# A gated delta layer of sixteen heads, worked in groups of four beside the next group's projections, with VectorE making the low parts of its weights

## The reference, cut to what matters

```python
def gated_delta_net(h, w_in, conv_w, a_log, dt_bias, norm_w, w_out):
    proj = h @ w_in
    qkv, z, b, a = jnp.split(proj, GDN_SPLITS, axis=-1)
    qkv = jax.nn.silu(causal_depthwise_conv(qkv, conv_w))
    ...
    q = l2_norm(q.reshape(B, T, GDN_K_HEADS, GDN_HEAD_DIM)) * GDN_HEAD_DIM ** -0.5
    k = l2_norm(k.reshape(B, T, GDN_K_HEADS, GDN_HEAD_DIM))
    ...
    o = chunk_gated_delta_rule(q, k, v, g, beta)
    o = rms_norm_2(o, norm_w) * jax.nn.silu(z.reshape(B, T, GDN_V_HEADS, GDN_HEAD_DIM))
    return o.reshape(B, T, GDN_V_W) @ w_out
```

## Time and profile before

| what | us |
|---|---|
| median of 3 runs | 3005.7 (3003.59 to 3010.06) |
| the profiled execution | 3002.97 |
| its span | 3001.2 |
| granted TensorE clock, mean | 0.909 |
| TensorE busy | 2625.9 (87%) |
| VectorE busy | 1721.6 (57%) |
| ScalarE busy | 1188.9 (40%) |
| GpSimd busy | 505.7 (17%) |
| HBM read | 340.86 MB, 114 GB/s over the span |

### The profile page before, as it was taken

The page is one execution under the profiler, slowest core; times in us unless marked ns, Lnnn a source line. Parts: engine busy times, 40 slices in busy tenths (PEclk is TensorE's granted clock), DMA queues, the critical chain, the costliest instruction groups (busy, mean ns, idle before and its releaser), DMA issues. The chain is left out here.

```text
span 3001.2 us, 49678 instructions
## 1 busy us (share of the span) xinstructions
PE 2625.9 (87%) x19342; PEld 2485.9 (83%) x19342; DVE 1721.6 (57%) x2747; ACT 1188.9 (40%) x1956; POOL 505.7 (17%) x400
## 2 busy tenths in 40 slices
PE   6998998996989788998999946989988788888998
PEld 6998888995987678997999844889888677778898
DVE  3677784665655444665566763466585733324665
ACT  2533554443444324442444442344444422223443
POOL 1110690000652000000000030000054221221000
PEclk9999799997999888999999966799998888878999
DMA  4465003553435421552455411235533200003453
GB/s 160 146 209 189 1 1 113 168 190 109 140 129 168 106 36 57 192 186 86 147 190 180 159 52 37 94 121 189 173 120 128 90 1 1 1 1 106 130 185 98
DMA packets 107153, 344.26 MB, mean 115 GB/s; under 512 B 20433, under 2 KB 26161, under 8 KB 106481
## 3 DMA queue, kind: packets, MB, share of 16 engines
q1 hardware_dynamic: 106992, 342.07, 35.2%
HBM read 340.86 MB, written 1.16 MB: 114 GB/s over the span
## 5 line engine op out<-in xcount | busy, mean ns | idle before, releaser
L134 PE MATMUL ps<-h_high,hi 128*128 128x256 f32 x2936 | 848.2, 289 | 59.9 <-DVE h_low L272 38.1
L111 DVE TENSOR_TENSOR lo<-raw,hi 128x1024 fp32r<-128x1024 f32 x537 | 655.6, 1237 | 321.1 <-ACT hi L101 320.6
L135 PE MATMUL ps<-h_low,hi 128*128 128x256 f32 x2936 | 838.9, 286 | 0.0
L136 PE MATMUL ps<-h_high,lo 128*128 128x256 f32 x2936 | 838.7, 286 | 0.0
L101 ACT ACTIVATE hi<-raw 128x1024 fp32r<-128x1024 f32 x623 | 646.4, 1054 | 463.8 <-PE ps L136 451.0
L134 PEld LDWEIGHTS ps<-h_high,hi 128*128 128x128 f32 x2936 | 571.7, 195 | 68.1 <-DVE h_low L272 41.6
L135 PEld LDWEIGHTS ps<-h_low,hi 128*128 128x128 f32 x2936 | 571.8, 195 | 2.0 <-issue 1.7
L136 PEld LDWEIGHTS ps<-h_high,lo 128*128 128x128 f32 x2936 | 571.4, 195 | 0.0
L134 PE MATMUL ps<-hidden_h,hi 128*128 128x256 f32 x1056 | 299.4, 284 | 9.8 <-DVE lo L111 9.4
L135 PE MATMUL ps<-hidden_l,hi 128*128 128x256 f32 x1056 | 298.0, 282 | 0.0
L136 PE MATMUL ps<-hidden_h,lo 128*128 128x256 f32 x1056 | 297.8, 282 | 0.0
(11 more groups left out here) (426 smaller groups left out, 4496.1 us busy)
## 6 DMA issues: line engine op xcount, KB each, us to landing
raw<-in_weights SPq DMA_DIRECT2D x623, 512.0 KB, 3.5
at_bias<-bias_group SPq DMA_DIRECT2D x64, 64.0 KB, 2.6
s_bn<-in_s_bn SPq DMA_DIRECT2D x4, 512.0 KB, 4.3
consts<-in_consts SPq DMA_DIRECT2D x1, 1794.5 KB, 8.8
x<-in_x SPq DMA_DIRECT2D x1, 1024.0 KB, 4.9
s_cT<-in_s_b SPq DMA_DIRECT2D x1, 1024.0 KB, 7.2
s_cw<-in_s_c SPq DMA_DIRECT2D x1, 1024.0 KB, 9.2
s_cT<-s_rows SPq DMA_DIRECT2D x16, 64.0 KB, 2.8
```

Of the source, the lines that this page charges most:

```text
L111: engine.tensor_tensor(k.lo[:, item % CUT, :], k.raw[:, item % RAW, :], k.hi[:, item % CUT, :].bitcast(F32), ALU.subtract)\
L134: pe.matmul(out, wh, xh, start=start, stop=False, **more)
L135: pe.matmul(out, wh, xl, start=False, stop=False, **more)
L136: return pe.matmul(out, wl, xh, start=False, stop=stop, **more)
```

## The change

`conv_silu`, `gdn_gates`, `L2Norms`, `head_norms` and the block of `delta_rule` become one block, `gdn_heads`. The weights are laid out in the order of `gdn_order()`: the 8 items of queries, keys and values of group 0 first, then 12 items for each of groups 0 to 2 (the next group's 8, and 4 for this group's z), then 4 for group 3. Only the first 8 are worked ahead of the delta rule. The other 40 are given out in the code by `some(fill, n)`, which issues the next n tiles of the projections (`KT` is 8, so an item, or half of one) between the delta rule's steps. VectorE takes every output tile (`taken`: `mixed` with the convolution, 5 instructions, or `gate`, 1) and makes every low part (`cut`). The query and key norms are folded into the columns of the decays (`columns`) as logarithms. The output norms are taken a group at a time inside the next group. Sizes, the arithmetic of a product, and the delta rule's matmuls stay.

```diff
+def gdn_order():
+    def mixed(g):
+        return [2 * g, 2 * g + 1, KT + 2 * g, KT + 2 * g + 1] + [GH + 4 * g + i for i in range(4)]
+    order = mixed(0)
+    for g in range(4):
+        order += (mixed(g + 1) if g < 3 else []) + [2 * GH + 4 * g + i for i in range(4)]
+    return order
...
-        @block.gpsimd
-        def _(pool):
-            for n in range(nt):
-                cut_item(k, pool, first + n)
...
+        def projected(a, b):
+            for m in range(a, b):
+                if m >= 8:
+                    pe.wait_ge(g.read, m - 1)
+                elif m >= 4:
+                    pe.wait_ge(g.read, m - 3)
+                for j in range(KT):
+                    mm = product(pe, k.ps[:, out_bank(m), 0:T], w.tile(m * ITEM + j), pair_tile(k.hp, j), start=(j == 0), stop=(j == KT - 1))
+                    if j == KT - 1:
+                        mm.then_inc(k.item_used, 1)
+                    yield
...
+        for hg in range(NG):
+            fill = projected(fill_at(hg), z_end(hg))
+            pe.wait_ge(g.cg, hg + 1)
...
+            some(fill, KT)
+            pe.wait_ge(g.v, hg + 1)
+            for a in range(2):
+                pe.wait_ge(g.t, U + a + 1)
+                pe.wait_ge(g.re, U + a + 1)
...
+                if a == 0:
+                    some(fill, KT)
             for l in levels:
...
+                some(fill, KT)
+                if hg and l == 3:
...
+                    head_sums(hg - 1)
+                if hg and l == 5:
+                    head_rows(hg - 1)
...
+            some(fill, KT // 2)
             for n in range(4):
...
+                    mm.then_inc(g.ws, 1)
+                    some(fill, KT // 2)
+                    pe.wait_ge(g.vn, 3 * hg + n)
...
+                if n == 1 and hg < NG - 1:
+                    square_sums(hg + 1)
+                some(fill, KT // 2)
+        head_sums(NG - 1)
+        head_rows(NG - 1)
...
+        def mixed(m):
...
+            dve.wait_ge(k.item_used, first + m + 1)
+            tapped(dve.tensor_tensor(cin[:, m % 2, 3:], k.ps[:, out_bank(m), 0:T], k.rs[:, 0, :], ALU.mult))
+            for s in range(4):
...
+                if s == 0:
+                    tapped(dve.tensor_scalar(acc, x, wc, None, ALU.mult))
+                elif s < 3:
+                    tapped(dve.scalar_tensor_tensor(acc, x, wc, acc, ALU.mult, ALU.add))
+                else:
+                    dve.scalar_tensor_tensor(dst, x, wc, acc, ALU.mult, ALU.add).then_inc(g.read, 1)
...
             for l in levels:
...
+                if hg and l == 4:
+                    head_variance(hg - 1)
+                if hg and l == 6:
+                    gates_scaled(hg - 1)
+                if more or l < 4:
+                    taken(F + l)
+                if l > 1 and (more or l < 6):
+                    cut(F + l - 2, F + l - 1)
+                if hg and l == 5:
+                    head_inverse(hg - 1)
...
+            if more:
+                taken(F + 7)
+                cut(F + 5, F + 6)
             for n in range(4):
...
+                if more:
+                    taken(F + 8 + n)
+                    cut(F + 6 + n, F + 7 + n)
```

More of the change, by code:

```diff
@@ L2018, with some @@
 LEVELS = 6
+def gdn_order():
[5 more added lines that the diff above has]
+    return order
+def some(fill, n):
+    for _ in range(n):
+        next(fill, None)
 def gdn(k):
     nc = k.nc
[L2023 to L2048, removed]
@@ L2049, in gdn @@
+    with ExitStack() as outer:
+        v = outer.enter_context(nc.sbuf_tensor("gdn_v", [P, GH, T], F32))
+        with ExitStack() as ctx:
+            gdn_heads(k, ctx, v)
         with nc.sbuf_tensor("gdn_vh", [P, 2 * KT, T], F32R) as vh, nc.sbuf_tensor("gdn_vl", [P, 2 * KT, T], F32R) as vl:
             linear(k, (vh, vl), 2 * KT, KT, parts=(Parts(k, v, (vh, vl), 2 * KT),), leave=True)
[L2053 to L2126, removed]
@@ L2335, in delta_rule, with gdn_heads @@
-def delta_rule(k, col, qk, v):
+def gdn_heads(k, ctx, v):
     nc = k.nc
@@ new lines, in gdn_heads, with four, q_of @@
+    v0, a0, i0 = V.n, A.n, k.side_here.n
+    prep = Prep(k, VEC_AT["norm_mix_pre_2"] + KT, Prep.POST, VEC_AT["norm_ffn_post_2"])
+    block = ctx.enter_context(nc.Block())
+    ident, cum = const(k, "ident"), const(k, "cumulate")
+    lmask = const(k, "levels").rearrange("p (l n) -> p l n", l=LEVELS)
+    dmask = const(k, "decay_mask")
+    levels = range(1, LEVELS + 1)
+    def four(bank):
+        return k.ps[:, bank, :].rearrange("p (h n) -> p h n", h=HG)
+    def q_of(hg, kh):
+        return qk[:, HG * (hg % 2) + kh, :]
@@ L2412, in _ @@
                     rows = slice(a * P, (a + 1) * P)
-                    if a == 0 and hg:
-                        pe.wait_ge(g.oc, 4 * hg)
+                    pool.wait_ge(g.re, U + a + 1)
                     for kh in range(2):
-                        for half, rhs in enumerate((k_of(hg, kh), q_of(hg, kh))):
-                            pe.matmul(k.ps[:, a, (2 * kh + half) * P:(2 * kh + half + 1) * P], k_of(hg, kh)[:, rows], rhs[:, rows],
-                                      start=True, stop=True)
@@ L2659, in build @@
+            for n in (1, 2):
+                pool.wait_ge(g.s, 3 * hg + n)
+                end = (n + 1) * GC
+                pool.tensor_tensor(Sd[:, :, :], S[:, n % 2, :, :], spread(rx[:, :, end - 1:end], 2, P), ALU.mult).then_inc(g.sd, 1)
+    A.n += 5
+    k.side_here.n += 48
+    k.used += n_out
 def build(nc, ins, x_in, out, plan, n_items):
```

1019 lines of the change are left out of this document (559 added, 460 removed).

## The result

| what | before | after |
|---|---|---|
| median, 4 runs each, same chip | 3007.07 (3003.59 to 3010.06) | 2920.24 (2913.36 to 2922.55) |
| the profiled execution | 3002.97 | 2921.78 |
| its span | 3001.2 | 2919.8 |
| granted TensorE clock, mean | 0.909 | 0.917 |
| TensorE, VectorE busy | 2625.9, 1721.6 | 2597.6, 1720.6 |

The ratio is 0.9708, 95% interval 0.9687 to 0.9728: 87 us less, where the prediction said 69 (it counts from the profiled execution, which lost 81). It lies in its range and in the case held likeliest. All of it is in the layer: of the profiled spans, 86.3 us fewer there and 4.9 more in the rest together. What stands ahead of the delta rule fell from 178.3 us to 39.2 (139.1 fewer). The four groups grew by 68.8 together, since 40 items and the norms of the heads now lie in them, and the tail fell from 30.1 to 14.2.

A forecast was written before the change was run, and what follows sets the result against it. Levels were held bound by TensorE, chunk steps by a serial chain on a slow TensorE. Front 42, groups 96.3, 198.6 and 87, tail 14, clock 18, contention 6: 461.9 against 531.3, so 2934 us; range 2905 to 2985.

The forecast's parts named there:

- the case held likeliest: The prediction's own case for the whole kernel: layer 461.9 against 531.3 us, time 2934; chance 0.52.
- contention: Groups: VectorE's low parts, both operands in SBUF, slowed beside GpSimd; 0 to 7 us a group, 2 taken, 6 in all.
- wait for the inverse: Level 5 to 6: TensorE waits 2.6 us as VectorE takes the norms' inverse behind updates, tile and low part.
- The path of TensorE: Groups 1 and 2 at full clock: TensorE's work from start to chunk steps summed to 99.3 us a group.
- +6 us for the clock: Chunk steps, groups 0 to 2: 5.6 us at half clock behind outputs and column sums; 6 a group, 18 in all.
- rival of cold steps: Chunk steps stay at the low clock in all groups, 24 us a group instead of 6: time 2988; chance 0.11.
- Waits of 1.1 a group: Chunk steps: 1.1 us of waits counted within their 29.8 us at full clock.
- The slack of 1.4 us: Levels 2 to 5: VectorE free 5.2 us after a level's last product, first needed 6.6 after it.
- The table loads: ScalarE: loads go from 8 to 22, at 1.28 us; by the skill's 2.66 a switch, about 5.5 us longer.
- Clock up: Rival: the clock stays up through the groups, saving the 18 us taken for it: time 2916; chance 0.17.
- Nothing hidden: Rival: VectorE's longer queue gives back to waits what items take out; layer 499 us, time 2971; chance 0.13.
- Slower: Rival: clock down through chunk steps and next starts, adding 54 and 42 us: time 3030; chance 0.05.

The follow-up runs named there:

- inverse-first run: Changed kernel with VectorE's inverse and ScalarE's root ahead of level 5's tile, low part and rounding: median 2915.9 us, 0.9694 of the kernel before; layer 436.8 against 445.0.
- bare steps: Changed kernel with the chunk steps' items moved in a row ahead of them: median 2970.5 us, 0.9869 of the kernel before; layer 495.0 against 445.0.
- twice-in-levels run: Changed kernel with the low part made twice in levels 2 to 4 of every group only: median 2922.9 us, 0.9705 of the kernel before; layer 447.6 against 445.0.
- twice-cut run: Changed kernel with every low part in the groups made twice, 2 to 8 us longer expected: median 2957.8 us, 0.9809 of the kernel before; layer 34 us longer.
- run with the items behind: Changed kernel with all items of a group behind its chunk steps, none between steps: median 3034.0 us, 1.0075 of the kernel before; layer 556.6 against 445.0.

## Why the prediction was right, and where it was off

**The sum.** 461.9 was predicted for the layer, 445.0 measured, 16.9 too much; the rest of the program took back 5 (2469.9 before, 2474.8 after, by the profiled spans). That the profiled time came within 12 us of 2934, and not 17, is luck. By parts:

| part | predicted | measured |
|---|---|---|
| front | 42 | 39.3 |
| group 0, with clock and contention | 104.3 | 99.3 |
| groups 1 and 2, each | 107.3 | 102.9 |
| of it: start | 14.2 | 14.1 |
| a level with its item | 8.45 | 8.30 |
| wait for the inverse | 2.6 | 2.2 |
| u, w and chunk steps | 33.7 + 6 | 38.5 |
| contention | 2 | 0 |
| group 3 | 87 | 86.5 |
| tail | 14 | 14.2 |

**The path of TensorE** was right to 0.2 us a level. Levels, start and tail came as summed, and the one new wait came where it was put, 2.2 for 2.6. The inverse-first run took it away whole.

**The chunk steps**, +6 us for the clock: right in kind and nearly in size. Clock 0.85, near the 0.8 that was said, down behind outputs and column sums and back with the next half item. But the prediction had one stretch of 5.6 us at half speed, and there are two, of 6.7 and 3.4, the second behind outputs alone; by them some 5 us are lost. The bare steps show the other side: steps at 0.58. They don't price the rival of cold steps, whose items stay in the steps: of their 16.8 a group, 11.5 are items moved out of cover, so that this is near that rival's 18 is chance. The Trainium skill (TensorE: Matmul & The Clock Gate, What's actually happening) has the clock follow how busy TensorE was; by the busy time of the records the trace still disagrees, since the steps at 0.85 were busy 33.37 of 33.37 us.

**Contention**, 2 us a group: this term was wrong. It was put on VectorE's low parts from the earlier trace rows. That instruction itself still takes 1.28 once a group, as before the change. Of the layer's low parts only three were slowed, to 1.36, 1.36 and 1.77 us. In the levels it is GpSimd that gives way: its masks start behind VectorE's low part, and two of them last 3.04 us where two alone are 2.14 (GpSimd's timeline, the same level as above):

```profile
2363.34 3.04 POOL L2707 TENSOR_TENSOR dr_mt<-dr_aq,consts 128x512 f32<-128x512 f32 x2 [1.93 <-PE ps L2287]
```

They are still in time, so nothing is paid. The Trainium skill (SBUF — State Buffer, SBUF: two separate sides) has the port that the two engines share go, for a whole instruction, to the one that starts first, the other waiting. The rows agree: the low part of 1.22 began 0.19 us before the mask, and the one of 2.00 during it. The twice-in-levels run shows that even a hit VectorE stays within the slack.

**The rest.** Waits of 1.1 a group that were kept for the chunk steps did not come, and the front was 2.7 shorter than VectorE's serial count.

**The slack of 1.4 us**, on which hiding rested, was right for the place it was worked out for (1.5 to 1.9 idle in the trace, and a whole further low part hidden). It was the expectation of the twice-cut run, not the prediction, that took it for the whole group, and it failed by 26 us or more. The prediction's own argument would have stood better with a slack for each part: none in the steps.

**The table loads.** A load takes 1.28 us and the next function starts 0.01 after it; the load itself starts 0.02 after the copy ahead of it has ended. The Trainium skill (ScalarE: Activation LUTs, What ACT_TABLE_LOAD costs) counts 2.66 a switch, which by the prediction's estimate would have made the layer 5.5 longer. The trace disagrees: the tail, with two loads in it, came at 14.2 for 14.

**The rivals.** Clock up (2916): the time was nearer to it than to 2934 in the profiled execution, yet the chunk steps show 0.85, not 1.0. What brought it near was the contention, the waits and the front, each put too high. Nothing hidden (2971): the run with the items behind comes nearest to that case, and its layer is 556.6 where the rival had 499. The rival left out that a row of items starts at the lower clock and is bound by VectorE in its convolved tiles, the serial chain at each group's end, and group 3's items in the tail (14 us). Slower (3030): cold steps and cold starts did appear together, in the bare steps, and cost 50 us there, 34.5 of it in the rows of items moved ahead of the steps; 8 of each group's 12 were still hidden.

## What to carry to other kernels

Lay independent dense products, half an item at a time, between the links of a serial chain: they fill its waits and bring TensorE's clock back, so that here three and a half items cost nothing where the chain alone had run at 0.58. Count the helper engine's slack for each place apart: one more low part in each of three levels was free, while more of them in the chunk steps were paid almost one for one (5.8 us of VectorE's time, 5.7 longer). Where a short instruction of one engine has a whole level of another queued behind it, issue it ahead of the long ones (2.2 us a group for two calls moved), and never let a new consumer wait for the producer of its own step when the one before is ready (5.11 against 3.68 us a tile).
